# Moving twelve row transfers of the final pass from the SyncE queue to the ScalarE queue in a fused decoder layer

## What is computed

```python
def mixer_output(x, oa, ob, ga, gb, p, w_out, g_ple, w_pg, w_ple):
    ...
    h = x + jnp.concatenate([ya, yb], axis=-1) @ w_out
    gate = jax.nn.sigmoid(rms_norm(h, g_ple) @ w_pg)
    return h + (p @ w_ple) * gate
...
y_prompt = rms_norm(xp, g_final)
y_sample = rms_norm(xs, g_final)
```

## Time and profile before

| what | value |
|---|---|
| median of three runs | 2419.85 us (2416.12 to 2421.75) |
| profiled execution, its own time | 2420.02 us |
| span of the profiled execution | 2418.2 us |
| TensorE busy | 97% of the span |
| VectorE, ScalarE, GpSimd busy | 35%, 28%, 32% |
| mean rate of all transfers | 122 GB/s over the span |

### The profile page before, as it was taken

One profiled execution on the slowest core, in us unless ns is written; L12 is line 12 of the kernel. 1 busy time (PEld: TensorE's weight loads), 2 busy tenths in 40 slices (PEclk: granted clock), 3 DMA queues, 4 the chain that ended last, 5 costly groups with the idle time before them and its releaser, 6 DMA issues.

```text
span 2418.2 us, 40441 instructions
## 1 busy us (share of the span) xinstructions
PE 2350.7 (97%) x16009; PEld 2227.5 (92%) x16009; DVE 853.3 (35%) x2328; ACT 669.6 (28%) x1985; POOL 765.8 (32%) x783
## 2 busy tenths in 40 slices
PE   5999999999999999999999999999999999999997
PEld 4999999999999999888878899999999999999997
DVE  7013323323323404555555525242122362211243
ACT  5122222222222313334545411120000132221444
POOL 2322222222222222222122233333333334454564
PEclk9999999999999999999999999999999999999998
DMA  5233234233233224444444354543232354333685
GB/s 189 68 111 98 75 109 101 76 110 98 78 110 101 78 94 124 137 132 137 135 138 145 115 164 134 166 136 104 87 99 79 124 158 128 104 109 106 179 242 189
DMA packets 383796, 294.26 MB, mean 122 GB/s; under 512 B 53807, under 2 KB 347927, under 8 KB 382319
## 3 DMA queue, kind: packets, MB, share of 16 engines
q1 hardware_dynamic: 342261, 249.43, 35.4%
q10 hardware_dynamic: 41347, 42.25, 5.2%
HBM read 225.38 MB, written 66.22 MB: 121 GB/s over the span
## 4 chain that ended last, share of the span: by engine, by line
PE 83%; DMA 6%; DVE 5%; ACT 2%; SPq 1%; POOL 1%; issue 1%; DVEq 0%; ACTq 0%; POOLq 0%
PE psum L1070 24%; PE psum L1072 23%; PE psum L1071 23%; PE psum L853 3%; PE psum L875 2%; PE psum L886 2%; PE psum L930 1%; DMA s_ring<-in_cache_a_k 1%; PE psum L945 1%; PE psum L958 1%; DMA y_in<-yt_scratch 1%; DVE x_n L1584 1%; PE psum L912 1%; POOL w_lo L809 1%; DMA w_raw<-in_w_ple 1%
## 5 line engine op out<-in xcount | busy, mean ns | idle before, releaser
L1070 PE MATMUL psum<-act_hi,w_hi 128*128 128x344 f32 x4032 | 1315.9, 326 | 4.3 <-POOL w_lo L809 2.7
L1072 PE MATMUL psum<-act_hi,w_lo 128*128 128x344 f32 x4032 | 1288.7, 320 | 0.0
L1071 PE MATMUL psum<-act_lo,w_hi 128*128 128x344 f32 x4032 | 1287.5, 319 | 0.0
L1070 PEld LDWEIGHTS psum<-act_hi,w_hi 128*128 128x128 f32 x4032 | 759.9, 188 | 15.0 <-issue 8.5
L1071 PEld LDWEIGHTS psum<-act_lo,w_hi 128*128 128x128 f32 x4032 | 759.3, 188 | 0.2
L1072 PEld LDWEIGHTS psum<-act_hi,w_lo 128*128 128x128 f32 x4032 | 759.0, 188 | 0.0
L807 POOL CAST w_hi<-w_raw 128x512 fp32r<-128x512 f32 (+1 forms) x352 | 221.0, 628 | 1544.1 <-PE psum L1072 1361.7
L809 POOL TENSOR_TENSOR w_lo<-w_raw,w_hi 128x512 fp32r<-128x512 f32 (+1 forms) x390 | 504.8, 1295 | 65.9 <-ACT w_hi L1523 37.6
L1667 DVE COPY prob_t<-psum 128x512 f32<-128x512 f32 (+1 forms) x56 | 35.5, 634 | 451.9 <-PE psum L886 451.9
L1934 DVE TENSOR_TENSOR t_gate<-psum,acc 128x344 f32<-128x344 f32 x48 | 24.8, 516 | 262.0 <-PE psum L1072 262.0
L1869 DVE TENSOR_TENSOR h_row<-psum,h_row 128x344 f32<-128x344 f32 x48 | 22.9, 516 | 242.4 <-PE psum L1072 230.8
(11 more groups left out here) (211 smaller groups left out, 2047.6 us busy)
## 6 DMA issues: line engine op xcount, KB each, us to landing
w_raw<-in_w_in SPq DMA_DIRECT2D x208, 256.0 KB, 3.1
w_raw<-in_w_pg SPq DMA_DIRECT2D x94, 256.0 KB, 3.0
w_raw<-in_w_out SPq DMA_DIRECT2D x64, 256.0 KB, 2.7
z_scratch<-stage ACTq DMA_DIRECT2D x72, 172.0 KB, 1.9
h_scratch<-h_row ACTq DMA_DIRECT2D x16, 516.0 KB, 2.7
x_in<-in_x_prompt SPq DMA_DIRECT2D x8, 1024.0 KB, 5.2
zq<-z_scratch SPq DMA_DIRECT2D x32, 256.0 KB, 3.9
o_scratch<-ot SPq DMA_DIRECT2D x32, 256.0 KB, 3.2
```

Of the source, the lines that this page charges most:

```text
L1070: pe.matmul(psum[:, bank, 0:T3], hi_w, hi_a[:, k, rows], start=(k == 0), stop=False, skip_group_check=True)
L1071: pe.matmul(psum[:, bank, 0:T3], hi_w, lo_a[:, k, rows], start=False, stop=False, skip_group_check=True)
L1072: return pe.matmul(psum[:, bank, 0:T3], lo_w, hi_a[:, k, rows], start=False, stop=stop, skip_group_check=True)
```

## The change

The twelve transfer pairs move from SyncE's program into ScalarE's. ScalarE issues `load_f(0)` to `load_f(5)` in its iterations u = 34 to 39 and `store_f(0)` to `store_f(5)` in u = 40 to 45, each behind `y_copy(u - 1)` and ahead of the rounding of the four gate2 groups. The waits move with them. SyncE keeps the loads of the weights and three small loads (`f_loaded6`) at n = 8, which take over the wait for `u_produced` and `y_stored`.

```diff
@@ sync
-                if n == 2:
+                if n == 8:
                     sp.wait_ge(sem("u_produced"), SECOND)
                     for par in range(2):
                         sp.wait_ge(sem(f"y_stored{par}"), 32 * ((SECOND + 1 - par) // 2))
-                if 2 <= n < 8:
-                    load_f(n - 2)
-                if n == 8:
                     for i in range(6, 9):
                         r0, rows = ROW_PIECES[i]
                         sp.dma_start(f_rows[i][0:rows, 0, 0:P], y_dram[r0:r0 + rows, 0:P]).then_inc(sem("f_loaded6"), 16)
-                if 7 <= n < 13:
-                    store_f(n - 7)
@@ scalar
+            def load_f(i):
+                r0, n = ROW_PIECES[i]
+                if i == 0:
+                    act.wait_ge(sem("u_produced"), SECOND)
+                    for par in range(2):
+                        act.wait_ge(sem(f"y_stored{par}"), 32 * ((SECOND + 1 - par) // 2))
+                if i >= 3:
+                    act.wait_ge(sem(f"f_loaded{i % 3}"), 32)
+                for out, rows in zip(cells(f_rows[i][0:n]), cells_of(y_dram[r0:r0 + n, :])):
+                    act.dma_start(out, rows).then_inc(sem(f"f_loaded{i % 3}"), 16)
+
+            def store_f(i):
+                r0, n = ROW_PIECES[i]
+                act.wait_ge(sem("f_scaled"), 2 * i + 2)
+                for rows, out in zip(cells(f_rows[i][0:n]), cells_of(yp[r0:r0 + n, :])):
+                    act.dma_start(out, rows).then_inc(sem("out_stored0"), 16)
@@ scalar, in the loop over u, behind y_copy(u - 1)
+                if 1 <= u - SECOND < 7:
+                    load_f(u - SECOND - 1)
+                elif 7 <= u - SECOND < 13:
+                    store_f(u - SECOND - 7)
                 if 1 <= u - SECOND + 3 < KT:
                     for part in range(4):
                         round_weights(u - SECOND + 3, part)
```

More of the change, by code:

```diff
@@ L745, in _ @@
                 sp.wait_ge(sem(f"h_stored{par}"), 16 * (KT // 2))
[L746 to L757, removed]
             for u in range(2):
```

## The result

| | kernel before | changed kernel |
|---|---|---|
| median (lowest to highest), 7 runs each | 2419.22 us (2414.54 to 2421.95) | 2427.43 us (2423.79 to 2436.73) |
| ratio to before, 95% interval | | 1.0039 [1.0021, 1.0057] |
| profiled execution | 2420.02 us | 2424.11 us |

By the medians the changed kernel is slower by 8.2 us (0.34%); the ratio, which is an estimate of its own, gives 0.39%, between 0.21% and 0.57%. The forecast of 2416.5 us had the wrong sign, and the time lies outside the range.

The account below looks back on a forecast made before the run. TensorE, busy 97%, bounds the kernel; at most 5.7 us of second-pass excess could return. Lateness 2.8 + 0.9 - 0.9 - 1.5 - 1.0 = 0.3 us; 2.2 us excess left, gain 3.5, hence 2416.5 us, range 2413.5 to 2424.0.

Parts of the forecast that it names:

- The weights have a queue of their own: Second pass: ple groups no longer stand behind row pieces in order; gain 1.0 us, bounds 0 to 2.9 us.
- The issue cost moves to ScalarE: ScalarE's loop, second pass: issuing each of twelve pairs adds 0.9 us between ple landing and next issue; upper bound 2.5.
- The ple group is issued later against its pair: Second pass: ple group follows the pair's start by 2.8 us instead of 1.92, so its landing time falls by 0.9 us.
- the prediction's sign for "right": Second pass ple landings: median near 4 us and none over 7.
- The doubled place goes: At n = 7, load and store no longer queue together ahead of a ple group; gain 1.5 us, bounds 0.6 to 3.1.
- ScalarE becomes the bottleneck: Rival: issue between `y_copy` and next rounding lengthens ScalarE's loops, up to 9 us more stops, 2429 us; chance 0.15.
- All stops vanish: Rival: in the second pass the loop keeps up everywhere and all 5.7 us come back, 2414.3 us; chance 0.25.
- nothing moves: Rival: ple group still waits for the piece beside it, stall moves by a unit, about 2420 us; chance 0.15.
- The prediction's first sign for "right": No unit of the second pass takes over 10 us.
- Its sign for "wrong": ScalarE waits in `store_f` for `f_scaled`, or a stop appears in units with stores, which had none except at 2344.

Follow-up runs that it names:

- the thirds on the two queues: Row pieces cut into column thirds spread between weight groups: kernel before, on SyncE's queue, 2415.4 us; changed kernel, on ScalarE's queue, 2419.8 us.
- the spread thirds: Kernel before, each row piece cut into thirds behind the ple and first two gate2 groups on SyncE's queue, stores later: 2415.4 us, 0.9981.
- the six pieces by rows: Changed kernel with each pair cut by rows into six transfers on ScalarE's queue, row pieces kept at 2752 and 2688 bytes: 2431.2 us, 1.0045.
- the run with small transfers: Kernel before plus two extra small transfers (12 KB together) issued by ScalarE at the pair's place in twelve iterations: 2419.6 us, 1.0007.
- the late run: Changed kernel with a wait ahead of each pair on ScalarE until GpSimd has split that iteration's ple group: 2429.0 us, 1.0047.

## Why the prediction was wrong

**The weights have a queue of their own** is the step that failed. It took 0 to -2.9 us for it and set -1.0. The sign was wrong. The step asked what a ple group gains that need not stand behind the pair in order, and bounded the answer by nothing at all on the bad side. It did not ask what happens to the gate2 groups. On SyncE's queue four of them a tile went ahead, the last of them 0.41 to 0.48 us before the pair, and landed in 2.6 to 4.9 us. The groups behind the pair were late, the ple group first (8.1 us, then gate2 groups of 7.6, 6.6 and 5.4 at the pair of 2300), but ScalarE asks for the ple group first, and by then the others are nearly there: 8.7 us of waits. From ScalarE's queue the pair starts among the gate2 groups: 7.4 and 6.9 us at the first pair, 7.7, 7.1 and 6.9 at the one of 2316. ScalarE's waits, 28.7 + 8.7 us before, are 0.7 + 58.5 us now.

Two things are mixed in this, and the prediction had priced neither for the gate2 groups: the place of the pair in the loop, and the queue. By the ratios, an estimate from runs that were not all made on one chip: from the stores one tile later (-0.12%) to the pair one place earlier on SyncE's queue (+0.20%) is 7.7 us; from there to the changed kernel (+0.39%), whose first pair stands at the same place, is 4.6 us. The first step is clear of its interval, the second is not by itself, but agrees with the 4.4 us between the thirds on the two queues. So the place seems at least as large a part as the queue. How they add up at each pair stays open, since the place shifts from pair to pair.

What such a landing may be can be worked out from rows the prediction had. A slot is filled again when its group is split, four groups later; a unit of 8.8 us uses five groups, so four take 7.0 us. Less 0.63 us of rounding and 1.27 us of split, 5.1 us are left for the landing. It is an estimate of what a group may take if all do. It does not sort the runs by their medians: the changed kernel's 5.6 us is over it and the spread thirds' 4.9 us under it, but the six pieces by rows have 4.4 us and an excess of 16.1, and the pairs early on SyncE's queue 3.5 us and 8.2. What stops TensorE is a few late groups and not the middle one; even the thirds have single landings of 6.3 us. The prediction made such a budget for the ple group only.

**The transfer engines are shared.** The gate2 landings of 7 to 8 us beside the pair show that the two queues share what moves the bytes. The Trainium skill, DMA: Bandwidth & Descriptors, section "Issuing engines are not separate DMA queues", says so, and its sentence that spreading the issue only saves the sequencer's time would have kept this step at zero, nearer to the result than -1.0; but no part of it says that the second queue costs something. The runs go beyond it: 8.2 us for the whole change, 4.4 between the thirds on the two queues. The turn by turn service between queues, told by the Trainium skill in "Queues, rings and completion order" on the same page, was read in the prediction as help for a short load behind a long one. No run here shows the turns themselves; if they are there, they work the other way as well, against the load that was issued first.

**The issue cost moves to ScalarE** was mis-sized. Taken were 0.9 us a pair in the loop. Two issues stand ahead of the execution and leave 0.7 us of waits in all; the run with small transfers measures 1.7 us for twelve (at most 4.4), where the sum took 0.9 for each loop. The gap of 0.82 us in the earlier trace rows stood behind `y_nat`, whose result those transfers store; here nothing just computed is waited for, which is the likely reason.

**The ple group is issued later against its pair** had the right sign: 3.45 us behind the pair's start where 2.8 was taken, because the pair goes out ahead of the row copies. The landings of ple groups reach 5.1 us at most, as the prediction's sign for "right" asked (none over 7), with a median of 4.7. But the same earlier start put the pair among the gate2 groups, and that was not priced.

**The doubled place goes** was taken at 1.5 us within 0.6 to 3.1. Alone it gives 3.8 us by the medians and 2.9 by the ratio (0.12%, from 0 to 0.24%), so the value is near the upper bound or above it, and the term was too small by about a half, as far as an interval that begins at nothing can tell.

**The rivals.** That ScalarE becomes the bottleneck had its time near the result, 2429 us, and the wrong mechanism: its price was the issue, which the small transfers refute. No rival had the pair delay the gate2 groups. "All stops vanish" and "nothing moves" did not happen. The prediction's first sign for "right", no unit over 10 us, was the one that failed plainly: six are. Its sign for "wrong", stops in the units with stores, came too: units u = 40, 43 and 45 take 10.49, 10.31 and 10.17 us.

## What to carry to other kernels

Before a bulk transfer is moved to a second queue, ask which loads now go just ahead of it and just behind it, and what they cost if they land late. On one queue, what stood ahead of the bulk here always had its 0.4 us of head start; on two queues it did not. Ask the same for the place in the loop, which on one queue alone was worth up to 8.5 us. Where the rate allows it, cut the bulk transfer and put the parts between the critical loads on the same queue; thirds took away every stop here. Give each group of a pipeline its own budget for landing, not only the one that is late now.

## What the runs showed of the hardware

ScalarE's transfers are issued ahead of its execution: a pair that stands behind three row copies in the program was issued 0.6 us and 0.2 us before the first of them began. Two issues an iteration cost 0.7 us of waits in the whole second pass, six cost 15 to 16 us.

A 256 KB load issued 0.01 to 0.04 us ahead of a pair of 704 or 1024 KB on another queue landed in 5.7 to 8.7 us (twelve times, in the late run). Issued 0.41 to 0.48 us ahead on its own queue it landed in 2.6 to 4.9 us in the kernel before (eleven times); issued 0.38 to 0.73 us ahead with the pair on the other queue, in 2.9 to 4.4 us in the changed kernel (five times).

Stages whose programs are alike put the start of the second pass 5 us apart in two executions, so the profiled times alone showed 4.1 us of the 8.2; the excess of the one stage showed 9.0.
